# FFN gate and up jobs paired, with seven block products for four of eight pairs of weight slices

## The reference, cut to what matters

```
FFN_HIDDEN = 5632
hf = rms_norm_2(x, g_ffn[layer])
x = x + (jax.nn.silu(hf @ w_gate[layer]) * (hf @ w_up[layer])) @ w_down[layer]
return rms_norm_2(x, g_final)
```

## Time and profile before

| | |
|---|---|
| median of 3 runs | 2502.28 us (2502.01 to 2502.35) |
| span of the profiled execution | 2499.9 us |
| TensorE busy | 2489.9 us, 11070 matmuls |
| VectorE busy | 1581.0 us |
| ScalarE busy | 1215.0 us |
| GpSimd busy | 192.0 us |
| mean granted TensorE clock | 0.999 |

### The profile page before, as it was taken

One profiled execution on the slowest core, in us unless ns is written; L12 is line 12 of the kernel. 1 busy time (PEld: TensorE's weight loads), 2 busy tenths in 40 slices (PEclk: granted clock), 3 DMA queues, 4 the chain that ended last, 5 costly groups with the idle time before them and its releaser, 6 DMA issues.

```text
span 2499.9 us, 29283 instructions
## 1 busy us (share of the span) xinstructions
PE 2489.9 (100%) x11070; PEld 2058.0 (82%) x11070; DVE 1581.0 (63%) x1974; ACT 1215.0 (49%) x1530; POOL 192.0 (8%) x319
## 2 busy tenths in 40 slices
PE   9999999999999999999999999999999999999998
PEld 7888788888888888888888889888888888888887
DVE  6665665665665666675767766686655555565556
ACT  6454444444555453444545556465544444444444
POOL 0010000000010100000001100010100000000000
PEclk9999999999999999999999999999999999999999
DMA  9676666666688877877678855675766666666664
GB/s 336 202 231 211 217 205 205 218 208 201 218 243 238 249 229 221 233 230 212 217 249 256 243 159 163 219 240 181 245 219 202 209 202 217 208 211 208 212 208 145
DMA packets 262428, 544.91 MB, mean 218 GB/s; under 512 B 13616, under 2 KB 19888, under 8 KB 261936
## 3 DMA queue, kind: packets, MB, share of 16 engines
q1 hardware_dynamic: 241152, 477.38, 59.2%
q0 software_dynamic: 21168, 66.08, 9.5%
HBM read 508.29 MB, written 35.13 MB: 217 GB/s over the span
## 4 chain that ended last, share of the span: by engine, by line
PE 99%; DVE 1%; ACT 0%; issue 0%; ACTq 0%; DVEq 0%
PE job L2043 32%; PE job L2044 31%; PE job L2049 31%; PE group L2067 1%; PE att L2316 0%; PE att L2088 0%; PE group L2338 0%; PE att L2213 0%; PE att L2317 0%; PE att L2101 0%; PE att L2102 0%; PE att L2098 0%; PE att L2198 0%; PE job L2450 0%; PE att L2081 0%; PE job L2451 0%
## 5 line engine op out<-in xcount | busy, mean ns | idle before, releaser
L1191 DVE TENSOR_TENSOR lo<-raw,hi 128x1024 fp32r<-128x1024 f32 (+1 forms) x880 | 1055.5, 1216 | 680.1 <-ACT hi L685 659.8
L685 ACT ACTIVATE hi<-raw 128x1024 fp32r<-128x1024 f32 (+1 forms) x880 | 922.1, 1055 | 1110.0 <-PE job L2049 1102.7
L2043 PE MATMUL job<-hi,xh 128*128 128x512 f32 (+1 forms) x2272 | 886.9, 391 | 0.3 <-ACT hi L685 0.3
L2044 PE MATMUL job<-hi,xl 128*128 128x512 f32 (+1 forms) x2272 | 881.2, 388 | 0.0
L2049 PE MATMUL job<-lo,xh 128*128 128x512 f32 (+1 forms) x2272 | 604.9, 388 | 0.0
L2043 PEld LDWEIGHTS job<-hi,xh 128*128 128x128 f32 x2272 | 426.7, 188 | 90.9 <-issue 2.3
L2044 PEld LDWEIGHTS job<-hi,xl 128*128 128x128 f32 x2272 | 426.5, 188 | 88.9 <-issue 2.1
L2049 PEld LDWEIGHTS job<-lo,xh 128*128 128x128 f32 x2272 | 425.4, 188 | 87.6
L2043 PE MATMUL job<-hi,ah 128*128 128x512 f32 x832 | 325.8, 392 | 0.0
L2044 PE MATMUL job<-hi,al 128*128 128x512 f32 x832 | 323.8, 389 | 0.0
L2049 PE MATMUL job<-lo,ah 128*128 128x512 f32 x832 | 222.5, 389 | 0.0
(11 more groups left out here) (328 smaller groups left out, 1218.1 us busy)
## 6 DMA issues: line engine op xcount, KB each, us to landing
raw<-in_ret_w_in SPq DMA_DIRECT2D x94, 1024.0 KB, 5.2
raw<-in_pool_w_in SPq DMA_DIRECT2D x64, 1024.0 KB, 6.2
raw<-in_w_gate SPq DMA_DIRECT2D x44, 1024.0 KB, 5.3
raw<-in_w_up SPq DMA_DIRECT2D x44, 1024.0 KB, 5.2
raw<-in_w_down SPq DMA_DIRECT2D x44, 1024.0 KB, 5.0
raw<-in_ret_w_out SPq DMA_DIRECT2D x32, 1024.0 KB, 5.1
raw<-in_pool_w_out SPq DMA_DIRECT2D x32, 1024.0 KB, 5.4
raw<-in_w_in SPq DMA_DIRECT2D x28, 1024.0 KB, 6.7
```

Source lines behind the costliest of these rows:

```text
L685: act.activation(hi[:, (U.at * 2 + h) % HS, :, 0:n], src, ACT.Copy).then_inc(hi_ready, 1)
L1191: dve.tensor_tensor(lo[:, (U.at * 2 + h) % LS, :, 0:n], src, hi[:, (U.at * 2 + h) % HS, :, 0:n].bitcast(F32), ALU.subtract).then_inc(lo_re ...
L2043: pe.matmul(o, oh[:, kt, ts], w, start=first and k == 0, stop=False)
L2044: pe.matmul(o, ol[:, kt, ts], w, start=False, stop=False)
```

## The change

Gate and up of a chunk are no longer two jobs of four units each. They become eight *pairs* v = 0 to 7; a pair is a unit that holds two slices of gate and the same two slices of up, loaded with two transfers of 512 KB, with a semaphore for each (`raw_landed`, `up_landed`). Gate and up then accumulate side by side in seven banks over all eight pairs. The hardware loop is written out as straight code.

A pair has the form of a 2 x 2 by 2 x 2 block product: two halves of tokens by two slices, times two slices by gate and up. The odd pairs do it with eight products (`plain_unit`); in its products with up the first half of the tokens is replaced by the difference of the halves. The even pairs (BILINEAR) do it with seven (`bilinear_unit`), 21 matmuls, in the manner of Strassen and Winograd. They need four sums of the weight blocks (`wsums`): VectorE makes the first two with one instruction, GpSimd makes the third and the fourth, one after the other (`late_sums`). ScalarE makes high parts of them two at a time (`high_sums`), VectorE low parts (`low_sums`). They also need sums of the token blocks (`tokens_made`, `tokens_high`, `tokens_low`), made once in eight steps, six or seven of them while chunk 0 runs. At the end of a chunk's pairs the banks are combined: `p1s` is copied by ScalarE, `partial_sums` and `gate_sums` on VectorE give gate and up in SBUF, Silu follows later, and `hidden` of chunk i is done in turn i+1 behind the low parts of v=1.

Kept as before: chunk 0, the down products, the closing stage.

```
+            def late_sums(i, v):
+                n, w = sums_at(i, v), four(ffn_at(i)[0] + v)
+                pool.wait_ge(sums13_made, n + 1)
+                if n:
+                    pool.wait_ge(sums_low, 2 * n)
+                pool.tensor_tensor(wsums[:, 2, :], wsums[:, 0, :], w[:, 3, :], ALU.add).then_inc(sum2_made, 1)
+                pool.wait_ge(sum2_made, n + 1)
+                pool.tensor_tensor(wsums[:, 3, :], wsums[:, 2, :], w[:, 1, :], ALU.add).then_inc(sum4_made, 1)
+            for i in range(1, FC):
+                for v in range(KV):
+                    if v in BILINEAR:
+                        late_sums(i, v)
+                    if v == 1:
+                        turn_across(NF + i - 1, fblk[:, :, :, :], fT[:, :, :])
+            turn_across(NF + FC - 1, fblk[:, :, :, :], fT[:, :, :])
...
# ScalarE, a turn
+                for v in range(KV):
+                    pair_high(U + v, i, v, 0)
+                    if v - 1 in BILINEAR:
+                        high_sums(i, v - 1, 1)
+                    pair_high(U + v, i, v, 1)
+                    if v in BILINEAR:
+                        high_sums(i, v, 0)
+                    if i == 1 and v < 2:
+                        tokens_high(6 + v)
+                    if v == 6:
                         hidden_high(I, ah)
...
# VectorE
+            def bilinear_low(U, i, v):
+                n, w = sums_at(i, v), four(U)
+                dve.wait_ge(raw_landed[U % RAW], (U // RAW).value(16, 16))
+                dve.wait_ge(up_landed[U % RAW], up_count(i, v))
+                if n:
+                    dve.wait_ge(sums_low, 2 * n)
+                dve.tensor_tensor(wsums[:, 0:2, :], w[:, 0:4:3, :], w[:, 2, :].unsqueeze(1).broadcast_to([P, 2, NB]),
+                                  ALU.add).then_inc(sums13_made, 1)
+                low_of(U, 0, slice(0, 2))
+                low_sums(i, v, 0)
+                low_of(U, 1, slice(1, 2))
+            def partial_sums(i):
+                dve.wait_ge(first_copied, i)
+                dve.wait_ge(seventh_done, i)
+                then(dve.tensor_tensor(u2[:, :], BANK6[:, :], p1s[:, :], ALU.add))
+                dve.tensor_tensor(u3[:, :], BANK7[:, :], u2[:, :], ALU.add).then_inc(seventh_read, 1)
+            def gate_sums(i, U_end):
+                wait_job(dve, U_end)
+                dve.wait_ge(seventh_read, i)
+                dve.tensor_tensor(sg[:, 0, :], BANK2[:, :], p1s[:, :], ALU.add)
+                dve.tensor_tensor(sg[:, 1, :], BANK4[:, :], u3[:, :], ALU.add).then_inc(gate_made, 1)
+                dve.tensor_tensor(fg[:, 1, :], BANK5[:, :], u3[:, :], ALU.subtract)
+                then(dve.tensor_tensor(u2[:, :], BANK5[:, :], u2[:, :], ALU.subtract))
+                dve.tensor_tensor(fg[:, 0, :], BANK3[:, :], u2[:, :], ALU.add).then_inc(up_made, 1)
+            def ffn_turn(i):
+                U, J, I = ffn_at(i)
+                for v in range(KV):
+                    if v in BILINEAR:
+                        bilinear_low(U + v, i, v)
                     else:
+                        low_of(U + v, 0, slice(0, 2))
+                        if v - 1 in BILINEAR:
+                            low_sums(i, v - 1, 1)
+                        low_of(U + v, 1, slice(0, 2))
+                    if v == 0 and i > 1:
                         accumulate(J - 1, U, 3)
+                    if v == 1:
+                        if i == 1:
+                            first_hidden()
+                        else:
+                            hidden(i - 1)
+                    if i == 1 and v < 2:
+                        tokens_low(6 + v)
+                        if v == 0:
+                            tokens_made(7)
+                    if v == 6:
                         hidden_low(I, al, ah)
+                U = U + KV
+                split_lo(U)
+                partial_sums(i)
+                split_lo(U + 1, halves=(0,))
+                gate_sums(i, U)
+                split_lo(U + 1, halves=(1,))
+                if i == FC - 1:
+                    hidden(i)
+                accumulate(J, U + 1, 0)
+                split_lo(U + 2)
...
# TensorE
+            def bilinear_unit(U, J, i, v):
...
+                wait_pair(U, 0)
+                if first:
+                    wait_drained(pe, J - (1 if i == 1 else 2))
+                    wait_drained(pe, J - (2 if i == 1 else 1))
+                ins = product(BANK1[:, :], xh[:, k, one], xl[:, k, one], hi[:, a, 0], lo[:, a, 0], first, last)
...
+                product(BANK2[:, :], xh[:, k + 1, one], xl[:, k + 1, one], hi[:, a, 1], lo[:, a, 1], opens, closes).then_inc(half_used, 1)
+                wait_pair(U, 1)
+                product(BANK3[:, :], sh[:, s, 3], sl[:, s, 3], hi[:, b, 1], lo[:, b, 1], opens, closes).then_inc(half_used, 1)
+                pe.wait_ge(sums_low, 2 * n + 1)
+                product(BANK5[:, :], sh[:, s, 1], sl[:, s, 1], wsh[:, 0], wsl[:, 0], opens, closes)
+                product(BANK7[:, :], sh[:, s, 0], sl[:, s, 0], wsh[:, 1], wsl[:, 1], first, last).then_inc(sums_used, 1)
+                pe.wait_ge(sums_low, 2 * n + 2)
+                ins = product(BANK6[:, :], sh[:, s, 2], sl[:, s, 2], wsh[:, 2], wsl[:, 2], first, last)
...
+                product(BANK4[:, :], xh[:, k + 1, two], xl[:, k + 1, two], wsh[:, 3], wsl[:, 3], opens, closes).then_inc(sums_used, 1)
```

More of the change, by code:

```diff
@@ L51 @@
 FC = FFN // NB
+KV = KT // 2
+BILINEAR = (0, 2, 4, 6)
 MLA_HEADS, MLA_NOPE, MLA_ROPE, MLA_V = 8, 128, 64, 128
@@ L579, in _ @@
                 load(Pos(OUT4_U + j), rows(w_xo[0], 0, NB * j))
[L581 to L602, removed]
@@ L1148, in kept_hi @@
+            for i in range(1, FC):
+                ffn_turn(i)
             def kept_hi(n):
@@ L1966, in kept_lo @@
+            wait_drained(dve, Pos(FJ))
+            for i in range(1, FC):
+                ffn_turn(i)
             def kept_lo(n):
@@ L2410, in _ @@
                     turn_x(Pos(OUT4_G), 0)
[L2413 to L2435, removed]
+            for u in range(4):
+                got = (Pos(OUT4_G), group_done) if u == 0 else (Pos(X_PARTS[3] + 2 * u), xt_low)
+                unit(Pos(FU + 2 * u), Pos(FJ), xh, xl, 4 * u, start=u == 0, stop=u == 3, groups=got[0], filled=got[1])
+                unit(Pos(FU + 2 * u + 1), Pos(FJ + 1), xh, xl, 4 * u, start=u == 0, stop=u == 3)
+            def product(o, oh, ol, wh, wl, start, stop):
+                pe.matmul(o, oh, wh, start=start, stop=False)
+                pe.matmul(o, ol, wh, start=False, stop=False)
+                return pe.matmul(o, oh, wl, start=False, stop=stop)
@@ new lines, in ffn_turn @@
+            def ffn_turn(i):
+                U, J, I = ffn_at(i)
+                if i == 1:
+                    pe.wait_ge(att_read, XA + 4)
+                    pe.wait_ge(group_done, OUT4_G + 2)
+                else:
+                    pe.wait_ge(up_made, i - 1)
+                for v in range(KV):
+                    if i == 1:
+                        pe.wait_ge(tok_low, v + 1)
+                    if v in BILINEAR:
+                        bilinear_unit(U + v, J, i, v)
+                    else:
+                        plain_unit(U + v, v)
+                U = U + KV
+                pe.wait_ge(t_low, I.value())
+                pe.wait_ge(first_copied, i)
+                for j in range(4):
+                    if j == 1:
+                        pe.wait_ge(seventh_read, i)
+                    unit(U + j, J + j, ah, al, 0, start=True, stop=True)
```

273 lines of the change are left out of this document (196 added, 77 removed).

## The result

The changed kernel takes 2568.4 us (median of 4 runs, 2566.0 to 2570.9) against 2502.3 us: a ratio of 1.0265, 95% interval 1.0251 to 1.0280. It is slower, as forecast; the predicted time was 2557 us, in a range of 2530 to 2595. The profiled execution's span is 2564.2 us, 64.3 us more than before.

A forecast was written before the change was run, and what follows sets the result against it. TensorE's matmuls were taken as the bound: -27.2 + 8.3 + 9 × (1.7 + 4.9) + 14 = +54.5 us on a 2499.9 us span, plus 2.4 us to the median, say 2557 us; range 2530 to 2595.

The forecast's parts named there:

- The gain: Four of eight pairs in ten turns do 21 matmuls in place of 24: 120 fewer, 27.2 us saved.
- Wait 1: At each turn's start TensorE waits for VectorE's accumulation of the last down job: 1.7 us lost, nine times.
- Wait 2: At v=2 of each turn, low sums come late because GpSimd's sums queue behind turn_across: 4.9 us lost, nine times.
- The first turn: At i=1, v=0, TensorE waits for first_hidden, which VectorE does in v=1: 8.3 us lost.
- The clock: Stalls of 4.9 us make the granted clock fall to 1.2 GHz: 1.4 us lost, ten times, 14 us.
- Rival B: GpSimd's sums and VectorE's two-SBUF-operand operations hold each other off: 3.3 us a turn, +33 us, 2590; 30%.
- rival A: The forecast itself, 50%; its own range runs from 2534 to 2565 us.
- C: GpSimd's queue is no bound: across transfer and sums quick enough, wait 2 gone, 2499 us; 6%.
- D: Faster: accumulation and Silu of the previous job come early enough, both waits vanish, 2475 us; 6%.
- E: Worse: the clock stays down between stalls, or half-size loads come late, up to 2640 us; 8%.
- The load of VectorE: VectorE's work in a turn comes to 55 us of 62.6; it fits in total, so order matters.

The follow-up runs named there:

- e1: Changed kernel with TensorE waiting for the previous turn's last down job just before the product into BANK7, no longer before unit 0: 2574.2 us.
- e2: Changed kernel with turn_across placed behind the sums of v=2 in GpSimd's order: 2539.9 us.
- e4: Changed kernel with VectorE making the third and fourth sums too, GpSimd only its transfers: 2522.8 us.
- e8: The mended kernel: changed kernel with e1's edit, VectorE's sums, first_hidden in v=0, and low sums ahead of the first weight low part in plain pairs: 2507.7 us.
- e10: e8 with hidden and its transposes moved from v=1 to v=3, hidden_high and hidden_low from v=6 to v=7: 2497.9 us.
- e3: Changed kernel with both the edit of e1 and the edit of e2: 2532.0 us.

## Why the prediction was right, point by point

**The gain** held: 120 matmuls less, and where nothing waits they come 0.2267 us apart, but for those on the sums of the weights (last section).

**Wait 1** was in its place with its releaser, but is 3.6 us and not 1.7. The step that was too small is "three steps of 1.15 and one of 0.6 bring it to about +0.2": the low sum took 2.24 and the half part 1.75 us, 2.1 us more. VectorE was done with v=0 at 2108.93, t = 2.2.

**Wait 2** was in its place too, behind the queue. I had it end at t = 20.2; it ended at 2127.52 - 2106.71 = 20.8, and between 20.8 and 22.1 over the nine turns. That its parts moved against each other is luck: the transposes ended at t = 9.5 and not 7.6, the four issues began 3.6 us after the first and not 5.27, and the sums took 1.3 us each as against 1.2. It lasts 1.8 us and not 4.9 because wait 1 and the slow unit 0 had eaten 1.9 + 1.8 us of it, against 0.6 by which it ended later. The forecast's 8.0 us a turn, 6.6 and 1.4 for the clock, became 20.8 - 60 x 0.2267 = 7.2 us, clock included, up to that point. That the two waits don't add is shown by e1: their sum is set by the later end.

**The first turn** lost 10.7 us against 8.3. Both `fg` ended at 1828.35 and not at 1825.6: the low part of v=0 was 1.2 us later than I had it already, and the rest is mostly the same two stretched instructions.

**The clock** was a step that went right in kind and not in size: 14 us were counted, about 24 measured. I had it fall once a turn behind wait 2. It falls around wait 1 in all nine turns, again behind wait 2 in three, mostly for 3.4 us each time, and stays down for 13.7 us in the first paired turn.

**Rival B** had 30% and was not the forecast, yet its mechanism is there in every turn. What it does to the time was over-priced at 33 us on top of the forecast: the result stands 11 us over it, since most of the delay fell into time that wait 2 would have taken anyway. So the forecast's sum came near with one cause missing, and that is in part luck. By the nine turns wait 2 was counted at 44 us and cost 19; wait 1 was counted at 15 and cost 32; with the clock's 10 us more these nearly cancel. Where the queue no longer hides it the contention comes out: 17.1 us between e2 and e4. A slip in rival A: its upper end of 2565 is counted from the span, and from the median it would be 2568. C, D and E didn't come about; the transfer did land sooner, at 3.6 us, but far from under 1.

**The load of VectorE** was called no bound: 55 us of 62.6. In the loop of the changed kernel VectorE was busy for 599.1 us, 59.9 a turn, about 7 of them the contention's delay (30 of the 40 pairs had it, at 2.2 us and little more), in turns of 70 us and more. In the mended kernel it has 57.1 us in a turn of 65.3. It was no bound by its sum in either, but how far it sets the last 1.6 to 2.7 us of a turn in e8 and e10 stays open.

## What to carry to other kernels

A saving on the engine that is always busy is worth its full price only if every helper can keep its order: price the last wait of each turn as an absolute time, since an earlier wait that is removed may only be waited later. Don't put a short operation that others wait for behind a blocking sequence of transfers in one queue, and before moving an addition from VectorE to GpSimd compare what it saves with what the exclusion costs. The seven-product form paid here where it stood away from the seams of a turn: two pairs gained 10.7 us, three with VectorE's sums 15.2; four lost in every form but the last, e10, which gained 4.1.

## What the runs showed of the hardware

- A 128x512 addition of two SBUF operands takes 1.3 us on GpSimd alone and 2.1 to 2.2 us beside VectorE's; VectorE's 1.22 us operation with two SBUF operands becomes 2.24, its 0.68 us one 1.75. Each waits for the end of the other's instruction. No run shows what happens to a VectorE operation with an operand in PSUM, since none fell beside a sum of GpSimd's.
- Behind or at the end of an idle time of 3.6 us the granted clock fell to 1.2 GHz in all nine turns, and 3.4 us passed in most of them before it was back, with matmuls 0.43 us apart. The same length of idle time did not always do the same: behind e4's nine waits of 2.4 us the clock fell four times, and in the changed kernel it fell behind waits of 1.9 and 2.0 us and not behind one of 2.3. In e3, where a single wait is at most 1.6 us in turns 2 to 10, no fall was seen.
- In the changed kernel matmuls on `wsh` and `wsl` started 0.234 us apart (nine steps from 2114.69 to 2116.80), others 0.2267. I have no experiment on the cause.
- Two things place the 7 us that the account left. The 12 such matmuls of 40 pairs cost 480 x 0.0077 = 3.7 us. The list of waits counts an idle time from the modelled end of the matmul before, 0.39 us after its start, though the next was due after 0.23; that is 0.16 us more for each of 19 waits, 3.1 us.
